# Second adaLN group of a hybrid decoder step, computed between the groups of the convolution projection

## What is computed

```python
def adaln(c, w_ada, b_ada):
    mod = jax.nn.silu(c) @ w_ada + b_ada          # 9 rows: 1 prompt, 8 samples; w_ada is 1024 x 6144
    return jnp.split(mod[:, None, :], 6, axis=-1) # sh1, sc1, g1, sh2, sc2, g2

q, kc_r, vc_r, ks, vs, kw, vw, gates, u, bg = project(modulate(x, ln1_g, sh1, sc1), ...)  # one projection
# project: the columns of attention, and three blocks of 512 columns hc, bg, cg of the convolution; u = cg * hc
o = nsa_attend(q, ...)       # compressed, selected and window branches
cy, conv_state = short_conv(u, state_conv, w_conv)
x = x + g1 * mix_out(o, bg * cy, attn_out_g, conv_out_g, w_o)
x = x + g2 * swiglu(modulate(x, ln2_g, sh2, sc2), w_gu, w_down)
```

## Time and profile before

| | us |
|---|---|
| median of 3 runs | 906.68 (905.94 to 906.79) |
| span of the profiled execution | 917.5 |
| PE busy | 851.0 (93%) |
| PEld busy | 725.8 (79%) |
| DVE busy | 624.0 (68%) |
| ACT busy | 374.3 (41%) |
| POOL busy | 307.3 (33%) |

### The profile page before, as it was taken

How to read it: one execution, slowest core, us unless ns; L and a number is a source line. 1 busy time by engine, 2 the same in 40 slices (tenths; PEclk the granted TensorE clock), 3 DMA queues, 4 the chain that set the end, 5 groups by cost and what they waited for, 6 DMA issues and landing times.

```text
span 917.5 us, 17109 instructions
## 1 busy us (share of the span) xinstructions
PE 851.0 (93%) x6685; PEld 725.8 (79%) x6685; DVE 624.0 (68%) x1220; ACT 374.3 (41%) x754; POOL 307.3 (33%) x303
## 2 busy tenths in 40 slices
PE   3499999999997789999999998999999999999998
PEld 2366778899994456776777798999999999888886
DVE  2146686388948674668485899988888888434444
ACT  1033262132135434866833664444444446323221
POOL 6456500000003311634400328766677773000000
PEclk9699999999998887999999999999999999999999
DMA  7988922237187987393102554333333324422201
GB/s 207 323 293 320 321 79 75 92 111 262 45 299 259 351 337 275 87 303 108 36 0 92 152 139 123 92 94 92 92 94 93 93 92 165 145 92 93 74 1 52
DMA packets 89167, 138.88 MB, mean 151 GB/s; under 512 B 9268, under 2 KB 59988, under 8 KB 84799
## 3 DMA queue, kind: packets, MB, share of 16 engines
q1 hardware_dynamic: 74866, 96.26, 32.6%
q0 software_dynamic: 9376, 40.31, 12.7%
q10 hardware_dynamic: 4844, 1.21, 0.6%
HBM read 130.58 MB, written 11.31 MB: 155 GB/s over the span
## 4 chain that ended last, share of the span: by engine, by line
PE 74%; DVE 10%; issue 8%; ACT 4%; POOL 2%; another core or an unknown queue 1%; DVEq 0%; POOLq 0%; ACTq 0%
PE bank L2445 17%; PE bank L2447 17%; PE bank L2446 16%; PE bank L2513 4%; PE bank L2439 4%; PE bank L2801 2%; PE bank L2474 2%; PE bank L2714 2%; PE bank L2933 2%; PE bank L2454 2%; PE bank L2455 2%; PE bank L2965 2%; PE bank L2771 1%; DVE ring_lo L535 1%
## 5 line engine op out<-in xcount | busy, mean ns | idle before, releaser
L2445 PE MATMUL bank<-s,ring_hi 128*128 128x288 f32 x620 | 184.1, 297 | 4.5 <-DVE ring_lo L535 4.5
L2446 PE MATMUL bank<-s,ring_lo 128*128 128x288 f32 x620 | 182.9, 295 | 0.0
L2447 PE MATMUL bank<-s,ring_hi 128*128 128x288 f32 x620 | 182.3, 294 | 0.0
L2445 PEld LDWEIGHTS bank<-s,ring_hi 128*128 128x128 f32 x620 | 116.2, 187 | 5.4 <-DVE ring_lo L535 5.3
L2447 PEld LDWEIGHTS bank<-s,ring_hi 128*128 128x128 f32 x620 | 116.8, 188 | 0.0
L2446 PEld LDWEIGHTS bank<-s,ring_lo 128*128 128x128 f32 x620 | 116.4, 188 | 0.0
L535 DVE TENSOR_TENSOR ring_lo<-mem,ring_hi 128x512 fp32r<-128x512 f32 x84 | 106.6, 1304 | 2.1 <-POOL mem L987 1.8
L535 DVE TENSOR_TENSOR dn_w<-wring,dn_w 128x2048 fp32r<-128x2048 f32 (+1 forms) x11 | 23.1, 2097 | 65.8 <-ACT dn_w L532 65.8
L2445 PE MATMUL bank<-dn_w,dn_hi 128*128 128x512 f32 x160 | 62.2, 389 | 0.0
L2446 PE MATMUL bank<-dn_w,dn_lo 128*128 128x512 f32 x160 | 62.2, 389 | 0.0
L2447 PE MATMUL bank<-dn_w,dn_hi 128*128 128x512 f32 x160 | 62.2, 389 | 0.0
(11 more groups left out here) (448 smaller groups left out, 2127.4 us busy)
## 6 DMA issues: line engine op xcount, KB each, us to landing
wring<-in_w_gu SPq DMA_DIRECT2D x44, 512.0 KB
wring<-in_w_ada SPq DMA_DIRECT2D x16, 1024.0 KB
wring<-in_w_in SPq DMA_DIRECT2D x10, 1024.0 KB
wring<-in_w_down SPq DMA_DIRECT2D x10, 1024.0 KB
wring<-in_w_ada SPq DMA_DIRECT2D x16, 512.0 KB
proj<-in_x_prompt SPq DMA_DIRECT2D x4, 512.0 KB
mem<-in_state_k_win POOLq DMA_DIRECT2D x8, 256.0 KB
mem<-in_state_v_win POOLq DMA_DIRECT2D x8, 256.0 KB
```

Source lines behind the costliest of these rows:

```text
L2445: pe.matmul(dst, sh, ml, start=first and k == 0, stop=False)
L2446: pe.matmul(dst, sl, mh, start=False, stop=False)
L2447: ins = pe.matmul(dst, sh, mh, start=False, stop=last and k == len(pairs) - 1)
```

## The change

Group 2 of adaLN is computed in the convolution projection. Its eight steps stand behind the chains (0, 1), (0, 2), (1, 0), (1, 1), (1, 2), (1, 3) and, two of them, (2, 0), by the table `ADA2_AT`; they leave the sample attention. It gets bank 7. `ada_rows(2)` moves from the fourth group of the sample attention to VectorE's work behind (2, 1). In the list of weight chunks blocks 0 and 1 stand between the weights of groups 0 and 1, blocks 2 and 3 between those of 1 and 2, blocks 4 to 7 behind those of 2, ahead of `pc`. In SP's program `done`, the point at which it turns from loads to stores, is behind the last `cv` chunk as it was, which now means behind blocks 0 to 3, too. The blocks 4 to 7 and `pc` are loaded behind the stores and the biases. The first four blocks of adaLN group 1 are loaded together, in the fourth round of the sample attention's row stores, and not two each in the third and fourth, where one at a time stood.

```diff
--- before.py
+++ after.py
@@ -58,6 +58,7 @@
 ADA_AT = {4: 0, 5: 1, 6: 2, 7: 3, 8: 4, 9: 5, 10: 6, 11: 7}
 
 
+ADA2_AT = {(0, 1): (0,), (0, 2): (1,), (1, 0): (2,), (1, 1): (3,), (1, 2): (4,), (1, 3): (5,), (2, 0): (6, 7)}
 ADA1_AT = {2: 0, 3: 1, 5: 2, 6: 3, 8: 4, 9: 5, 11: 6, 13: 7}
 
 X_AT = {8: (0, 1), 9: (2, 3), 10: (4,)}
@@ -213,7 +214,7 @@
         if s == MOD_TURN:
             low_ring.append(("mod", 1))
     wide += [("pO", t) for t in range(4)]
-    extra += [("ada", 2), ("ada", 1)]
+    extra += [("ada", 1)]
     before = len(ring)
     ring += [("wo", 0, 0), ("wo", 0, 1), ("oT", 4), ("ss", 3)]
     ring += [("wo", 0, t) for t in range(2, 5)]
@@ -229,6 +230,7 @@
     at, used = {}, [0] * 8
     for keys, banks in ((start, (0, 1, 2, 3, 4, 5, 7)), ([("ada", 0)], (6,)), ([("cmp", 15)], (7,)),
                         ([("in", n, t) for n in range(3) for t in range(5)], range(8)),
+                        ([("ada", 2)], (7,)),
                         (ring[:pairs], (0, 1, 2, 3, 4, 5)), (ring[pairs:before], (0, 1, 2, 3, 4)),
                         (low_ring, (0, 1, 2, 3, 4)), (extra, (5,)),
                         (ring[before:], (0, 1, 2, 3, 4, 5)), (wide, (6, 7))) + tuple(([k], (b,)) for k, b in last):
@@ -244,9 +246,11 @@
 
     c = [(("ada", 0, kk), None) for kk in range(8)]
     c += [(("in", n, kh), None) for n in range(3) for kh in range(2)]
-    c += [(("cv", n, kh), None) for n in range(3) for kh in range(2)]
+    for n in range(3):
+        c += [(("cv", n, kh), None) for kh in range(2)]
+        c += [(("ada", 2, kk), None) for kk in range(2 * n, 2 * n + 2 if n < 2 else 8)]
     c += [(("pc", x, 0), None) for x in range(2)]
-    c += [(("ada", g, kk), None) for g in (2, 1) for kk in range(8)]
+    c += [(("ada", 1, kk), None) for kk in range(8)]
     c += [(("wo", n, kh), ("wo", max(n, kh), 4)) for n in range(2) for kh in range(2)]
     c += [(("gu", f, 0), None) for f in range(NFT)]
     c += [(("dn", n, kc), None) for n in range(2) for kc in DN_KC[n]]
@@ -758,7 +762,7 @@
                 sp.dma_start(arows[p0:p0 + w // 16, at0:at0 + 512],
                              bass.AP(a["b_ada"].tensor, c0, [[512, w // 512], [0, 32], [1, 512]])).then_inc(bias_loaded, 16)
 
-            done = chunk_of["pc", 0, 0]
+            done, after = chunk_of["cv", 2, 1] + 1, chunk_of["ada", 1, 0]
             for t in range(5):
                 if t < 2:
 
@@ -793,12 +797,10 @@
                 count += store(o["s_v_win"][0, b, SEQ - NQ:SEQ].rearrange("q k d -> q (k d)"),
                                pj[NQ * b:NQ * b + NQ, 4, TVW:TVW + 128])
 
-            for i in range(done, done + 2):
-                load(i)
             want_filled(sp, ("sconv",))
             for piece in range(1, 4):
                 bias(piece)
-            for i in range(done + 2, done + 6):
+            for i in range(done, after):
                 load(i)
             sp.wait_ge(nrm_done, 11)
             for c0, name in ((TKS, "p_k_slc"), (TKW, "p_k_win")):
@@ -813,8 +815,9 @@
             assert count == N_STORED
 
             for gp in range(4):
-                for i in range(done + 6 + 2 * gp, done + 8 + 2 * gp):
-                    load(i)
+                if gp == 3:
+                    for i in range(after, after + 4):
+                        load(i)
                 sp.wait_ge(o_row, gp + 1)
                 sp.dma_start(o_rows[2 * gp:2 * gp + 2].rearrange("b h q n -> (b h q) n"),
                              orows[:, 192 * gp:192 * gp + 192]).then_inc(rows_out, 16)
@@ -831,7 +834,7 @@
                 sp.wait_ge(x1_ready, 5 + t + 1)
                 sp.dma_start(x1_rows[128 * t:128 * t + TM[t], :], xin[t][0:TM[t], :]).then_inc(x1_first_out if t < 2 else x1_out, 16)
 
-            for i in range(done + 14, g0 + 1):
+            for i in range(after + 4, g0 + 1):
                 load(i)
             for t in range(4):
                 x1_store(t)
@@ -1875,6 +1878,8 @@
                     turn_chunks(17)
                     both_chunks(16)
                     cmp_scores(0)
+                    dve.wait_ge(bias_loaded, 64)
+                    ada_rows(2)
                 if m == 2:
                     both_chunks(17)
                     cmp_probs(0)
@@ -2024,8 +2029,6 @@
                     queries_low(0)
                     cmp_masked(0)
                     cmp_shifted()
-                    dve.wait_ge(bias_loaded, 64)
-                    ada_rows(2)
                 if more:
                     turn_window(gp + 1)
                     cmp_importance(gp + 1)
@@ -2659,6 +2662,8 @@
                         fills(products(ps(key)[:, 0:HALF], [((wv[0][:, k, f:f + 128], wv[1][:, k, f:f + 128]),
                                                              (h1hi[k][:, cols], h1lo[k][:, cols])) for k in range(8)],
                                        True, True), key)
+                    for kk in ADA2_AT.get((n, m), ()):
+                        ada_step(2, kk)
                     if n == 2:
                         if m in (1, 2):
                             compress_first(15 + m)
@@ -2856,8 +2861,6 @@
                     turn_probs(gp, 4, 6)
                     if gp == 0:
                         sum_conv()
-                    for kk in range(2 * gp, 2 * gp + 2):
-                        ada_step(2, kk)
                     cmp_values(gp + 1)
                     if gp == 1:
                         turn_blocks(2)
```

## The result

The changed kernel takes 949.3 us (median of 4 runs, 947.8 to 951.1) where the kernel before takes 906.3 (4 runs, 905.2 to 906.8): a ratio of 1.046, interval 1.043 to 1.049, 43 us longer. The forecast was 929 with a range of 914 to 937: the sign was right, the size was not, and the range didn't hold the time.

The account below looks back on a forecast made before the run. TensorE was taken to bound the projection, the sample attention having gaps and a full DMA. 8.5 + 12 + 2 + 5 - 1.8 - 4.5 + 1 = +22.2 us gave 929 us, range 914 to 937.

Parts of the forecast that it names:

- Which stage is the bound: Projection: TensorE has no gaps and DMA to spare, so the eight moved steps lie wholly on the path, +8.5 us.
- The frame and SP's order: Projection: third group's weights wait until 226.1, block 4 is issued from 240.5 and wanted by TensorE at 242.5.
- The wait for block 4: Before the fifth step: block 4 lands behind the window copies at 254.5, so TensorE waits +12 us.
- The clock: Projection, after the wait for block 4: some 4 us of work at half speed, +2 us.
- Blocks 6 and 7: End of the projection's steps: ring slots wait for the last split, 3.5 and 1.6 us of waiting, +5 us.
- The sample attention: Gives back 1.8 us for steps and 4.5 for loads gone; loading four later blocks together costs +1.
- The sum: Whole kernel: all terms add to +22.2 us on the profiled 917.5, so 939.7 there and 929 us timed.
- more is lost: Rival: second wait also slows the clock, no unnamed wait goes, value pages and block 7 late; 940 us, chance 0.13.
- not slower: Rival: saturated DMA truly bounds the sample attention, which gains 18 us against 16.5 in the projection; 905 us, chance 0.05.

Follow-up runs that it names:

- c2: e1 with steps 6 and 7 behind chains (2, 1) and (2, 2), block 4 loaded before the stores, block 5 before the bias, keys before blocks 6 and 7: 919.3 us.
- c3: c2 with the two sample-window copies moved behind the last load of the output projection: 910.8 us.
- g1: The changed kernel with the window copies issued late and blocks 4 and 5 loaded ahead of the three bias transfers: 917.9 us.
- g2: The changed kernel with only blocks 4 and 5 loaded ahead of the bias transfers, the window copies left where they are: 937.3 us.
- after: The changed kernel itself, without any follow-up edit: 949.3 us.
- e1: The changed kernel with the two sample-window copies issued behind the loads of blocks 4 to 7 and the compressed keys: 930.7 us.
- c1: e1 with steps 6 and 7 behind chains (2, 1) and (2, 2) and the bias added behind (2, 3): 932.7 us.
- f1: The kernel before with group 2's steps 64 columns wide instead of 512, so its gates are wrong: 2.9 us gained by the medians.
- f2: The kernel before with each of group 2's 16 loads cut from 1024 to 128 columns, gates wrong: 7.2 us gained by the medians.
- b1: The kernel before with only the two window copies moved behind the last load of the output projection: 906.7 us.
- g3: e1 with the three bias transfers written as eight, one for each row of 512 numbers, in the same place: 924.4 us.

## Why the prediction was wrong, step by step

- **Which stage is the bound.** Right. The projection has no gap to take eight steps, and these cost 8.5 us: the first two thirds of c2, c3 and g1 are 5.9 to 6.3 us longer than those of before for six steps, where nothing waits.
- **The frame and SP's order.** Right, once the 12.9 us by which the projection starts earlier are taken off. Third group's weights: forecast 226.1, so 213.2, seen 213.41. The step for block 4: forecast 242.5, so 229.6, seen 257.31 - 27.26 = 230.05. Block 4's issue: forecast 240.5, so 227.6; SP came to the bias at 226.08, and with the 1.77 us that this took before that is 227.85. That the issue itself would hold SP until 240.99 wasn't forecast.
- **The wait for block 4: this is the step that failed**, 12 us forecast, 27.3 measured. That block 4 waits behind the copies was right; two terms of it were not. The copies: 12 forecast, 18.0 measured alone (g2). The 2.7 to 4 us in which block 4 follows them were right (3.8 in g2), the end of the copies was not. I took it to be at 226 us in before, because the rate changes behind it, so at 251, which is 238.1 in after; it was at 244.1. In before they really ran until 232.3: the 337 GB/s of 228 to 230 are the copies with smaller transfers beside them, on the engines that they leave free. Of the packets that start from 226 to 232 us in before, ten are over 8 KB, and these are the last of the 64 of the copies:

```profile
DMA packets 413, 1.07 MB, mean 178 GB/s; under 512 B 156, under 2 KB 212, under 8 KB 403
```

The bias: nothing forecast, 9.3 of the wait with the copies ahead (27.3 less 18.0) and 10.2 without (10.5 less 0.3). So 12, 6 for the end of the copies and 9.3 for the bias make the 27.3. I had counted its three transfers as 1.77 us of SP's time, and never asked how long they lie on the DMA. The windows on which I rested it stop at 230 us and go on at 252; from 236 to 240, behind the same bias transfers, the trace of before shows a share of 0.13 and 50 GB/s, with nothing queued behind. So the kernel before has this tail already, and there it costs nothing:

```profile
236.00:238.00 2.00, 1.00 0.13 50
238.00:240.00 2.00, 1.00 0.13 51
```

- **The clock.** +2 us forecast. The first two thirds are 35.6 us longer: 6.4 of steps, 27.3 of waiting, so 1.9 for the clock, about the 2 of the forecast although the wait is twice as long. In the last third TensorE is busy 37.65 us and not 32.19; 2.1 of the 5.5 are two steps, the other 3.3 the slow clock (0.93 on average) after the waits for blocks 6 and 7, of which I had none. Together 5.2 in place of 2.
- **Blocks 6 and 7.** Right: 3.5 + 1.6 forecast, 3.89 + 1.93 measured, and nearly the same in e1 (5.9 together). The compressed keys came late, as said, and cost nothing in after: VectorE waited 7.6 us for them, TensorE didn't. In c1, where VectorE waited 9.0 us for them, TensorE did wait, 7.5 us.
- **The sample attention.** Right in direction and nearly in size: -1.8 for the steps (f1, timed: -1.0 to -4.2 for seven eighths of their products, and nothing in the stage itself), -4.5 for the loads (f2: -6 to -7 timed, -5.1 in the stage, for seven eighths of the bytes), +1 for the loads of group 1, which no run takes by itself. Measured for the whole: -4.4 to -7.3 in after, -7.6 in c3 (against b1). The stage has a lower clock in after (0.78) than in c3 (0.84), which may be why after gets less; this wasn't tried.
- **The sum.** Steps 8.5, three waits 33.1, clock 5.2, other idle time -0.5: 46.3, where I had 8.5 + 17 + 2. The rival "more is lost" (940) had the right sign for the wrong reasons; no rival had a second thing in the queue. The range was too narrow because its upper end was made of the terms that I had, each a bit larger.
- **The rival "not slower"** (905) needs all waits gone. c3 has that in the projection, and comes to 910.8: its projection is 10.8 us longer (8.5 of steps, 0.8 of waiting; the other 1.5 go with a clock of 0.96 in the last third, but weren't taken apart), its sample attention 7.6 shorter. So in the best placement that was tried the change doesn't pay.

## What to carry to other kernels

Before you load something behind other transfers of a queue, list all that stands ahead of it there with its bytes and with how many engines of the DMA each one uses, not only how long its issue takes. A stretch with a low, constant DMA share (here 0.13 and 0.50) was a transfer on few engines; it was free as long as nobody stood behind it, and what was left of it was owed as soon as somebody did. Take such a share over a stretch much longer than one packet, and take the end of a transfer from its packets, not from a change of the rate: other transfers beside it change the rate, too. And moving a long transfer out of the way moves the stall to the next one that is close to its deadline (here blocks, then compressed keys, then cache pages): look at who is issued behind its new place.

## What the runs showed of the hardware

- Bias transfers of 128 KB, whose source has an outermost size of 2, moved about 50 GB/s at a share of 0.13, and a block of 1 MB over all engines, queued behind them and one of 256 KB with a size of 4, was there 13.9 us after its issue (e1). With the same bytes in eight transfers with an outermost size of 32, the halves of the blocks landed in 5.1 us (g3; 11.4 in e1, medians).
- Two copies of 2 MB within DRAM, with an outermost size of 8, ran at 216 GB/s and a share of 0.50 (after, 228 to 242.4 us). Loads over all engines behind them got half of their packets through at once and the other half only when the copies ended (g2).
- SP was held for 13.63 us in the issue of a 128 KB transfer, behind two copies of 2 MB within DRAM (the three bias transfers together: 14.86 us in after, 8.0 with the copies cut finer, 1.82 without them ahead). In e1 a 17.66 us issue of a small store stands behind the copies in their new place.
- With block 4 behind the bias, the DMA stood at a share of 1.02 to 1.04 and moved only 259 to 277 GB/s, where the same blocks moved at 381 to 408 with nothing slow ahead. Each packet took longer: share times 16 engines times 2 us, divided by the packets of 2 KB and more, is 225 ns in e1 and 167 in g3 (both 234 to 236 us). Why they do wasn't settled.
